# GpSimd sums the squares of two norms for TensorE

## The reference

```python
def rmsnorm(x, g):
    xf = x.astype(jnp.float32)
    y = xf * lax.rsqrt(jnp.mean(xf * xf, axis=-1, keepdims=True) + EPS)
    return (y * g.astype(jnp.float32)).astype(x.dtype)
```

```python
x = x + memory_cross_attention(rmsnorm(x, norm_xq[l]), rmsnorm(mem, norm_mem[l]), ...)
...
h = rmsnorm_2(x, norm1_w[l])
x = x + mixer(h, w_in[l], ret_gn_w[l], conv_w[l], w_o[l])
```

## Time and profile before

| | |
|---|---|
| median of three runs | 1724.62 us (1723.93 to 1724.96) |
| profiled execution, its own time | 1722.8 us |
| its span, first to last instruction | 1721.0 us |
| PE, weight loads of PE, DVE, ACT busy | 78%, 61%, 38%, 28% of the span |
| POOL busy | 0.2 us, four instructions |
| transfers | 517 MB, mean 301 GB/s |
| mean granted clock of TensorE | 0.914 of full speed |

### The profile page before, as it was taken

The page is one execution under the profiler, slowest core; times in us unless marked ns, Lnnn a source line. Parts: engine busy times, 40 slices in busy tenths (PEclk is TensorE's granted clock), DMA queues, the critical chain, the costliest instruction groups (busy, mean ns, idle before and its releaser), DMA issues.

```text
span 1721.0 us, 31237 instructions
## 1 busy us (share of the span) xinstructions
PE 1346.2 (78%) x13674; PEld 1057.5 (61%) x13674; DVE 653.4 (38%) x1011; ACT 487.9 (28%) x799; POOL 0.2 (0%) x4
## 2 busy tenths in 40 slices
PE   7998899989899999998866656665756575667665
PEld 6988889989799999987543333333423342333333
DVE  6685735758797768584110001010101010110002
ACT  4764356446554445442100000000000000000001
POOL 0000000000000000000000000000000000000000
PEclk9999999999999999998998889788988888888888
DMA  7532022444255554478999999999999999999995
GB/s 288 172 123 96 27 97 101 148 172 147 99 211 183 185 190 153 148 296 360 423 430 432 428 433 430 430 427 433 430 431 427 432 428 430 431 430 431 429 433 231
DMA packets 37078, 517.28 MB, mean 301 GB/s; under 512 B 4114, under 2 KB 4242, under 8 KB 5138
## 3 DMA queue, kind: packets, MB, share of 16 engines
q1 hardware_dynamic: 37010, 516.32, 73.8%
HBM read 515.25 MB, written 1.05 MB: 300 GB/s over the span
## 4 chain that ended last, share of the span: by engine, by line
PE 43%; DMA 40%; DVE 11%; ACT 3%; issue 2%; SPq 0%; another core or an unknown queue 0%; DVEq 0%; ACTq 0%
DMA e_gu<-experts 39%; PE psum L305 9%; PE psum L307 8%; PE psum L306 8%; PE psum L800 7%; DVE all_sq L1375 3%; DVE w_low L1421 3%; PE psum L836 3%; PE psum L367 1%; PE psum L514 1%; ACT w_high L908 1%; PE psum L498 1%; PE psum L842 1%; DVE f_y L1759 1%; PE psum L809 0%
## 5 line engine op out<-in xcount | busy, mean ns | idle before, releaser
L800 PE MATMUL psum<-e_gu,x_xt 128*32 128x256 f32 x3072 | 206.0, 428 | 156.8 <-DMA e_gu<-experts 142.2
L305 PE MATMUL psum<-h_high,w_high 128*128 128x256 f32 x928 | 266.3, 287 | 14.2 <-DVE w_low L1421 8.9
L307 PE MATMUL psum<-h_high,w_low 128*128 128x256 f32 x928 | 262.8, 283 | 0.0
L306 PE MATMUL psum<-h_low,w_high 128*128 128x256 f32 x928 | 262.7, 283 | 0.0
L800 PEld LDWEIGHTS psum<-e_gu,x_xt 128*32 128x32 f32 x3072 | 105.6, 123 | 250.3 <-DMA e_gu<-experts 158.3
L1421 DVE TENSOR_TENSOR w_low<-w_raw,w_high 128x2048 fp32r<-128x2048 f32 x101 | 230.7, 2288 | 44.3 <-ACT w_high L908 38.3
L908 ACT ACTIVATE w_high<-w_raw 128x2048 fp32r<-128x2048 f32 x101 | 193.0, 1913 | 73.0 <-PE psum L307 61.9
L305 PEld LDWEIGHTS psum<-h_high,w_high 128*128 128x128 f32 x928 | 177.0, 191 | 17.2 <-DVE w_low L1421 10.2
L1997 DVE COPY x_yb<-psum 128x256 f32<-128x256 f32 x64 | 27.2, 425 | 418.8 <-PE psum L836 418.8
L306 PEld LDWEIGHTS psum<-h_low,w_high 128*128 128x128 f32 x928 | 177.1, 191 | 0.4 <-issue 0.2
L307 PEld LDWEIGHTS psum<-h_high,w_low 128*128 128x128 f32 x928 | 176.9, 191 | 0.0
(11 more groups left out here) (427 smaller groups left out, 2129.9 us busy)
## 6 DMA issues: line engine op xcount, KB each, us to landing
e_gu<-experts SPq DMA_DIRECT2D x48, 4096.0 KB, 52.9
e_dn<-experts SPq DMA_DIRECT2D x64, 2048.0 KB, 49.9
w_raw<-dense SPq DMA_DIRECT2D x101, 1024.0 KB, 4.8
e_gu_lo<-experts SPq DMA_DIRECT2D x16, 2048.0 KB, 47.4
e_gu_hi<-experts SPq DMA_DIRECT2D x16, 2048.0 KB, 51.8
all_c<-c SPq DMA_DIRECT2D x1, 2048.0 KB, 15.9
r_c<-c SPq DMA_DIRECT2D x1, 1344.0 KB, 5.9
all_x<-x_t SPq DMA_DIRECT2D x1, 1024.0 KB, 4.9
```

The lines of the kernel that those rows point to most:

```text
L305: mm(ps, w[0], src[0], start=start, stop=False, **kw)
L306: mm(ps, w[0], src[1], start=False, stop=False, **kw)
L307: return mm(ps, w[1], src[0], start=False, stop=stop, **kw)
L800: last = mm(half(psum[32 * s:32 * s + 32, GU_BANK[j % 2], 0:256], P), X["xt"][:, k, CAP * j:CAP * (j + 1)], expert_gu(j, k)[:, :, s * P:(s ...
```

## The change

For the norms `mem` and `n1`, GpSimd waits for the second pair of squares and adds it to the first pair in place, then the third and the fourth. Each add covers two chunks, 128x512 elements, and waits for the one before it. PE waits for the third add and multiplies only the two chunks that hold the sums. The other five norms stay as they were.

```diff
+        SUMMED = ("mem", "n1")
+        def summed(name, q):
+            return 3 * SUMMED.index(name) + q
...
             def mean_square(name, first=0, last=DC):
+                if name in SUMMED:
+                    ps = aux.fill(pe, f"ms_{name}")
+                    pe.wait_ge(sem("sq_summed"), summed(name, 3))
+                    for k in range(2):
+                        ins = mm(ps[:, 0:T], C("inv1024"), sq[:, k, :], start=(k == 0), stop=(k == 1))
+                    aux.filled(ins, f"ms_{name}")
+                    return
...
+        @block.gpsimd
+        def _(pool):
+            for name in SUMMED:
+                for q in (1, 2, 3):
+                    pool.wait_ge(sem("squares"), quarter(name, q))
+                    if q > 1:
+                        pool.wait_ge(sem("sq_summed"), summed(name, q - 1))
+                    nc.gpsimd.tensor_tensor(sq[:, 0:2, :], sq[:, 0:2, :], sq[:, 2 * q:2 * q + 2, :],
+                                            ALU.add).then_inc(sem("sq_summed"), 1)
```

## The result

| | before | changed |
|---|---|---|
| median (range) | 1724.63 us (1721.95 to 1724.97), 8 runs | 1730.03 us (1727.85 to 1733.75), 8 runs |
| ratio | 1 | 1.0038, 95% interval 1.0029 to 1.0047 |
| profiled execution, its own time | 1722.8 us | 1728.74 us |

The change makes the kernel slower, by 5.4 us. The prediction said 1722.7 us, with 1721.5 to 1727.8 as its range, so the time lies outside it, on the slow side.

What follows compares the result with a forecast made beforehand. The dense part was taken to set the pace, its events releasing SP's expert transfers. Gains of 1.5 us in mem and 0.4 in n1, 1.9 off the median of 1724.62, gave 1722.7 us; range 1721.5 to 1727.8.

Steps and rivals of the forecast that it cites:

- mem, the adds: Memory norm: three GpSimd adds in a row would keep PE waiting only 0.1 us.
- G: Time of one GpSimd add of 128x512, taken as 1.4 us, between 0.69 and 3.35.
- mem, the cap: Memory norm: DVE's low part moves the reciprocal by only 0.85 us, so mk0 starts 1.5 us earlier, not 2.3.
- From there the shift is whole: After mk0, through the xq norm: mem's gain of 1.5 us is passed on in full.
- a moved spell: Forecast gain plus a lower-clock spell spared by the shift, making it faster by over 0.2%; chance 0.02.
- a gain of 0.4: n1: q21 starts at 668.57 instead of 668.96, 0.4 us earlier, and the root stays.
- 3G - 2.15: n1: PE's wait for the three adds in us, 2.05 with an add of 1.4 us.
- the rival with a chance of 0.33: n1: adds and DVE's `w_low` exclude each other; PE idles 5.8 us, 1.9 us slower overall, 1726.5 us; chance 0.33.
- The lost clock in n1: n1: PE's long idling may also lower the granted clock, priced by an earlier spell that lost some 1.5 us.
- the worse half of the case: n1: exclusion of adds and `w_low` with lost clock on top, 1728.0 us instead of 1726.5.
- The gain that does not arrive: Downstream of the norms: a DVE or SP step sets the pace, time stays at 1724.6 us; chance 0.09.

Runs made afterwards that it cites:

- e1: Changed kernel with GpSimd adding the squares of mem only, n1 as before: 1723.82 us, ratio 0.9996.
- e3: Changed kernel with 22 superfluous PE passes put ahead of PE's wait in n1: 1727.36 us, ratio 1.0019.
- e4: Changed kernel with DVE waiting for n1's third add before it makes `w_low` of q21 and k20: 1724.65 us, ratio 1.0005.
- e6: Changed kernel run again without an edit: 1730.56 us, ratio 1.0036.
- e9: Adds for mem only, with superfluous PE products filling gaps of the cross attention: 1723.27 us, ratio 0.9995.
- e12: Changed kernel with superfluous PE passes both in n1's wait and in the cross attention's gaps: 1724.73 us, ratio 1.0006.
- e7: Adds for mem only, with DVE making mk0's low part between the sixth and seventh chunk of the normalisation: 1724.13 us, ratio 1.0003.
- e5: Kernel before the change, run again without an edit: 1723.77 us, one run.
- e2: Changed kernel with GpSimd adding the squares of n1 only, mem as before: 1727.11 us, ratio 1.0023.
- e8: Adds for mem only, with three superfluous DVE additions of two SBUF tensors beside them: 1724.81 us, ratio 1.0004.
- e11: Adds for mem only, mk0's low part made early and the cross attention's gaps filled with superfluous PE passes: 1721.39 us, ratio 0.9985.
- e10: Kernel before the change, with superfluous PE products filling gaps of the cross attention: 1724.63 us, ratio 1.0002.

## Why the prediction was wrong, step by step

**mem, the adds: right.** G was taken as 1.4 us with a lower end of 0.69 and an upper one of 3.35; it is 1.26 to 1.31, spaced by 1.44 (three adds in 4.16), so a hand-over between two adds is 0.14 us and not the 0.25 taken. The first add in e1 starts 6.05 us behind out01 (predicted 6.1), PE does not wait, and the first GpSimd instruction of its kind has no extra start-up cost. The figure worked out from the Trainium skill (GPSIMD Engine Reference, section Performance versus the Vector engine) was 1.12 us, an estimate by proportion; the trace has 1.30.

**mem, the cap: right.** The reciprocal was to move by 0.85 and moved by 0.93, and mk0's `w_low` was to leave 1.5 us of the gain. The stage gained 1.61 in e1, e3, e4, e6, e9 and e12. e7 lifts the cap and gets 2.57.

**"From there the shift is whole": wrong.** This is the first step that failed. Six profiles have mem's stage earlier and the cross attention as it was (changed, e6, e1, e3, e4, e7). All six show PE at the half clock near 450 us (in e4 only from 452 to 456) and lose 1.2 to 2.5 us there. The four that have it no earlier, or by 0.16 us at most (before, e5, e2, e8), show no spell. In that stretch PE stands again and again, as its waits from 440 to 460 us in the changed kernel say:

```profile
PE psum L670 <- ACTq L1068: 4.3, 4, 1.7
PE psum L662 <- DVE m_s L1751: 1.4, 1, 1.4
```

The kernel before has the same waits, 4.3 and 1.4 us. When the stretch falls on the trace's own clock does not decide: the reciprocal of xq is at 404.70 in before, without the spell, and at 404.77 in e1, with it. With the gaps filled the spell does not come (e9, e11, e12), so the spell needs them. Why 1.6 us earlier is enough to bring it on isn't shown. I had given a moved spell 0.02, and only as a gain.

**n1, "a gain of 0.4": wrong, and the larger part.** The wait was to be 3G - 2.15, which is 1.8 us with the measured G. It was 4.7. The formula had no term for DVE. The two `w_low` of the earlier trace rows fall into the adds, and add and `w_low` exclude each other. Against the squares the root came 2.5 us later, where no move was forecast, and q21 3.0 us later, where 0.4 earlier was. That was the rival with a chance of 0.33, and its order of events came true step by step: add after the first `w_low`, second `w_low`, second add, third add. It priced the idle time at 5.8 us with G = 1.4, and it was 4.7: the blocked adds end only 1.12 to 1.16 us after `w_low` (0.5 of the difference), the second `w_low`, the third add and the releases are 0.5 us shorter in all, and PE came 0.16 us later. Less the 12 passes saved (2.44) that is 2.2 us, and the stage in e3 and e12 shows 2.25 and 2.24. The row of before that should have changed the odds was there. DVE reads two SBUF operands for 4.6 us between 662.26 and 667.74, and none beside the adds of mem. (In the earlier trace rows a wait of 0.2 us for `cat_low` was passed over; nothing hangs on it.)

The Trainium skill (SBUF — State Buffer, section Who interferes with whom) says that a vector instruction with two SBUF inputs and a GpSimd one that reads SBUF contend, and the second to issue is blocked fully. The traces agree: e4 and e8 switch the effect off and on, with 1.3 against 2.1 to 3.1 us an add.

**The lost clock in n1: right in kind, a little too small.** The rival had 1.5 us for it; e2 and e6 against e3 give 1.6, the changed kernel 2.0. It came on top in all three profiles with the unfilled stall, where I had made it the worse half of the case.

**The sum.** -1.61 for mem, +1.9 for the spell near 450 us, +2.25 for the stall, +1.6 for the clock behind it: +4.1 us, and e6's first three stages give the same. The medians have +5.4 (interval 5.0 to 8.1) and +6.8 (4.3 to 8.1). The 1.3 to 2.7 us between are open. The last stage is where profiles vary, by -0.4 to +3.6 us against before, for kernels that are the same from 740 us on. DVE's reciprocal in the router (`x_r`, L1969 at 809.75 before, L1994 at 819.46 in e6) splits it. From the group norm to there, before and then e6:

```profile
738.57:809.75 71.18, 61.64 (x418) 56.35 (x417) 43.23 (x87) 23.09 (x30) 0.00 (x0) 0.90 0.84 340
```

```profile
744.47:819.46 74.99, 65.46 (x418) 59.34 (x417) 43.21 (x87) 23.10 (x30) 0.00 (x0) 0.84 0.80 322
```

PE does the same work, with the same waits in its list, and is busy for 3.8 us more at a lower clock. That is the whole +3.60 of e6: a third place where clock is lost. The changed kernel's first profile has 71.21 us there, so not every execution has it. Over all profiles this part is as long as before, to 0.1 us, at a mean clock of 0.90, 0.9 us longer at 0.88 (e3, e4, e7, e8), 1.6 at 0.86 (e9) and 3.8 at 0.84. Behind the reciprocal five profiles have 2.1 to 2.6 us more than before (e1, e4, e7, e10, e12) and all others -0.5 to +0.7, whatever the change. The two fastest executions of e6, 1725.79 and 1726.13 us, had a mean clock of 0.911 and 0.913, the other six, 1729.68 to 1732.24 us, 0.905 to 0.910. Whether the change makes these losses more frequent stays open: one or two profiles for a kernel can't say it. SP starts its first expert transfer 5.5 us later in the changed kernel (755.32), of which 1.7 is the later start of out01.

**The gain that does not arrive.** In e1, up to the group norm, no new wait took the gain of mem: it was PE's clock. So this rival, given 0.09, was half true for mem, by another mechanism than the one named.

## What to carry to other kernels

Before work is given to GpSimd, lay its instructions over DVE's timeline: where a two-operand SBUF instruction of DVE meets one, the later of the two waits for all that is left of the earlier, and an order of a single wait (e4) can remove it. An engine relieved of 2.4 us is worth what the next late producer leaves (here 1.5 to 1.6), and a cap like that can be lifted for nothing (e7). When a saving vanishes, compare the granted clock stretch by stretch before looking for a wait: two spells at half clock, 200 us apart, cost 3.5 us here, and a few superfluous products that cost 0.26 us kept one of them away.

## What the runs showed of the hardware

- The exclusion is counted in the blocked instruction's own duration and not as idle time before it: a DVE sum of 128x1024 is 1.23 us free and 2.33 behind an add, an add of 128x512 is 1.30 free and 2.1 to 3.1 behind DVE. A busy share of POOL or DVE thus holds waiting.
- A stretch of PE that repeats to 0.02 us between executions can fall to the 1.2 GHz level when the work ahead of it comes 1.6 to 2.9 us earlier: between 448 and 457 us the granted clock came down to 0.50 in six of six such profiles and stayed at 1.00 in four of four others.
- A wait of 4.7 us cost PE 1.6 to 2.0 us more behind it, at clock 0.50, and none when 22 passes filled it.
